# One core, two transformer blocks in float32r: regrouped weight transfers, thin stages as one tile, later turns of x, a reordered stretch of the latent attention, and another matmul order in three tiles

## The reference, cut to what matters

```
mh = rmsnorm(mem, mem_norm);  mk, mv = split(mh @ w_mem_kv)     # first block, memory branch
h  = rmsnorm(x, attn_norm);   proj = h @ w_in ...
u  = causal_dwconv(h2 @ w_up);  x = x + (silu(g) * val) @ w_down
# GLA: q, k, v, gate, gk_low = split(h @ w_in);  gk = gk_low(16 columns) @ w_gk2 + b_gk
# MLA:
proj = h @ w_in                              # 512 | 512 | 64 | 2048 columns
c_q, c_kv, k_rope, gate = split(proj)
q  = (rms_norm(c_q)  @ w_qb ).reshape(S, 16, 128 + 64)    # q_nope | q_rope
kv = (rms_norm(c_kv) @ w_kvb).reshape(S, 16, 128 + 128)   # k_nope | v
q_rope = rope(q_rope);  k_rope = rope(k_rope)
out = causal_softmax(q k) v * silu(gate) @ w_out
```

## Time and profile before

| | us |
|---|---|
| median of 3 runs (2471.82 to 2472.93) | 2472.68 |
| the profiled execution: its own time | 2475.55 |
| its span | 2473.8 |
| TensorE busy in it | 2444.2 (99%) |
| VectorE busy | 1495.6 (60%) |
| ScalarE busy | 1235.7 (50%) |
| mean granted TensorE clock | 0.996 |

### The profile page before, as it was taken

The page is one execution under the profiler, slowest core; times in us unless marked ns, Lnnn a source line. Parts: engine busy times, 40 slices in busy tenths (PEclk is TensorE's granted clock), DMA queues, the critical chain, the costliest instruction groups (busy, mean ns, idle before and its releaser), DMA issues.

```text
span 2473.8 us, 34147 instructions
## 1 busy us (share of the span) xinstructions
PE 2444.2 (99%) x12328; PEld 2070.6 (84%) x12328; DVE 1495.6 (60%) x1842; ACT 1235.7 (50%) x1588; POOL 32.2 (1%) x59
## 2 busy tenths in 40 slices
PE   8999999999999999999999999999999999999998
PEld 7888888888888888888888888888878788789987
DVE  5654544456695565777557765776545555666564
ACT  6544444554445444555445544555454444546553
POOL 2000000000000000000000000000000000000000
PEclk9999999999999999999999999999999999999999
DMA  8565666556566655666666666656655566464554
GB/s 262 175 187 151 205 185 192 160 180 190 161 190 184 211 183 186 184 187 191 195 188 186 185 192 192 185 181 188 173 165 162 178 188 193 124 188 131 159 175 158
DMA packets 421879, 448.29 MB, mean 181 GB/s; under 512 B 30533, under 2 KB 284601, under 8 KB 421250
## 3 DMA queue, kind: packets, MB, share of 16 engines
q1 hardware_dynamic: 419794, 440.80, 59.3%
q0 software_dynamic: 1936, 5.91, 0.9%
q10 hardware_dynamic: 32, 0.01, 0.0%
HBM read 444.55 MB, written 2.10 MB: 181 GB/s over the span
## 4 chain that ended last, share of the span: by engine, by line
PE 94%; DVE 2%; ACT 2%; DMA 1%; SPq 1%; issue 1%; DVEq 0%; ACTq 0%
PE blk L641 88%; PE pa L894 1%; DMA weight_raw<-in_w_mem_kv_dram 1%; DVE weight L1749 1%; ACT weight L1169 1%; PE pa L702 1%; SPq L496 1%; PE pa L679 0%; PE pa L1013 0%; PE pa L693 0%; DVE arena L1749 0%; PE pa L704 0%; PE pa L773 0%; PE pa L791 0%; PE pa L711 0%
## 5 line engine op out<-in xcount | busy, mean ns | idle before, releaser
L1749 DVE TENSOR_TENSOR weight<-weight_raw,weight 128x1024 fp32r<-128x1024 f32 (+2 forms) x840 | 1006.2, 1205 | 736.7 <-ACT weight L1169 732.9
L1169 ACT ACTIVATE weight<-weight_raw 128x1024 fp32r<-128x1024 f32 (+2 forms) x840 | 869.5, 1042 | 747.4 <-PE blk L641 693.6
L641 PE MATMUL blk<-weight,h 128*128 128x512 f32 (+1 forms) x4632 | 1044.6, 386 | 1.5 <-DVE weight L1749 1.5
L641 PEld LDWEIGHTS blk<-weight,h 128*128 128x128 f32 x4632 | 857.1, 188 | 173.9 <-DVE weight L1749 1.9
L641 PE MATMUL blk<-u,weight 128*128 128x512 f32 x3808 | 673.6, 338 | 1.4 <-DVE weight L1749 1.4
L641 PEld LDWEIGHTS blk<-u,weight 128*128 128x128 f32 x3808 | 580.9, 188 | 89.2 <-DVE weight L1749 1.8
L641 PE MATMUL blk<-weight,u 128*128 128x512 f32 x1920 | 448.9, 394 | 1.2 <-DVE weight L1749 0.8
L641 PEld LDWEIGHTS blk<-weight,u 128*128 128x128 f32 x1920 | 361.7, 190 | 78.7 <-DVE weight L1749 2.6
L641 PE MATMUL blk<-h,weight 128*128 128x256 f32 (+1 forms) x896 | 137.5, 316 | 0.8 <-DVE arena L1811 0.8
L641 PEld LDWEIGHTS blk<-h,weight 128*128 128x128 f32 x896 | 124.8, 190 | 13.2 <-DVE weight L1749 1.0
L1749 DVE TENSOR_TENSOR arena<-arena,blk 128x512 f32<-128x512 f32 (+2 forms) x69 | 46.9, 679 | 53.9 <-ACT arena L1542 31.7
(11 more groups left out here) (252 smaller groups left out, 957.2 us busy)
## 6 DMA issues: line engine op xcount, KB each, us to landing
weight_raw<-in_w_in_dram SPq DMA_DIRECT2D x208, 512.0 KB, 3.7
weight_raw<-in_w_up_dram SPq DMA_DIRECT2D x344, 256.0 KB, 3.2
weight_raw<-in_l_gla_w_in_dram SPq DMA_DIRECT2D x96, 512.0 KB, 4.2
weight_raw<-in_w_down_dram SPq DMA_DIRECT2D x84, 512.0 KB, 4.3
weight_raw<-in_w_branch_dram SPq DMA_DIRECT2D x48, 512.0 KB, 4.2
weight_raw<-in_l_mla_w_in_dram SPq DMA_DIRECT2D x48, 512.0 KB, 4.4
weight_raw<-in_w_mem_kv_dram SPq DMA_DIRECT2D x32, 512.0 KB, 5.1
weight_raw<-in_w_out_dram SPq DMA_DIRECT2D x32, 512.0 KB, 4.2
```

Of the source, the lines that this page charges most:

```text
L641: mm = nc.tensor.matmul(to, lhsT, rhs, start=(kt == 0 and m == 0), stop=(kt == ph.bt - 1 and m == len(ops) - 1))
L1169: nc.scalar.activation(hi, raw, ACT.Copy).then_inc(hi_made, 1)
L1749: return nc.vector.tensor_tensor(out_, a, b, op)
```

## The change

- **Transfers.** `heads_from` gives one transfer for all heads of a k chunk: two per tile in place of eight (`qrope`) or four (`v0`, `v1`). The pieces keep their sizes, 256 and 512 bytes.
- **Thin stages.** `decay` and `krope` are one tile of 16 chunks each, and one transfer each. ACT no longer waits, at the start of a thin stage, for the block before it.
- **x turned later.** The turns of x, and their splits, move from steps 0 to 3 of `memv` to steps 2 to 5 (on ACT and DVE 1 to 4 becomes 3 to 6), the norm of `mem_k` three steps later; the turn of `mem_k` stays at step 13.
- **Latent stretch.** `krope` moves behind `qnope0`. The side work is spread anew (below). The evictions of `qnope` and `knope` move from DVE (`copied_to`) to ACT (`columns_to`). `latent`, its junk and `k_rope`/`k_raw` get other places in `arena`.
- **Matmul order.** In the first tile of `sbqk`, `up1` and `up2` (`twos=True`) the matmuls of two chunks are grouped: hi, hi, lo, lo in place of hi, lo, hi, lo. For this the first round of these stages' loop is written out.

```
-        Phase("sbqk", "fm", 8, K16, TC, cols_from(win, 0, K16), "copy"),
+        Phase("sbqk", "fm", 8, K16, TC, cols_from(win, 0, K16), "copy", twos=True),
...
+            Phase(f"up{f}", "fm", nf, K16, TC, pair_from(wup, K16, c0 * P, DFF + c0 * P, P), twos=f > 0),
...
-        Phase("decay", "fmp", 1, K16, DECAY_RANK, cols_from(gla_w_in, 3 * D, K16, DECAY_RANK)),
+        Phase("decay", "fmp", 1, [KD], DECAY_RANK, cols_from(gla_w_in, 3 * D, [KD], DECAY_RANK)),
...
-        Phase("krope", "fmp", 1, K16, LR, cols_from(mla_w_in, 2 * LRANK, K16, LR), "copy"),
...
+        if r == 0:
+            phases += [Phase("krope", "fmp", 1, [KD], LR, cols_from(mla_w_in, 2 * LRANK, [KD], LR), "copy")]
...
-            return [(slice(width * h, width * h + width),
-                     w3[:, 2 * kt:2 * kt + 2, bass.ds(b * (n * per_head) + (first + h) * per_head + at, width)])
-                    for h in range(n)]
+            return [((k, width), w4[:, 2 * kt + k, bass.ds(b * n + first, n), at:at + width]) for k in range(2)]
...
+                        if two_by_two:
+                            ops = [ops[2 * k + m] for q in range(0, nk, 2) for m in range(2) for k in (q, q + 1)]
...
                 steps(pe, plan, ph, 0, side is not None, tile,
-                      from_round=int(ph.t0 == 0 or x_wait is not None))
+                      from_round=int(ph.t0 == 0 or x_wait is not None or ph.twos))
...
             def side_memk(j):
-                if j < 4:
-                    if j == 0:
+                if 2 <= j < 6:
+                    r = j - 2
+                    if r == 0:
                         norm_at(pe, "x", "hn", NT)
...
-            project(PH["krope"], u, side=lambda j: None)
+            project(PH["qrope"], h, x_wait=norm_ready("qa"), side=lambda j: None)
+
+            def side_qnope(j):
+                if j == 1:
+                    turn_latent(1)
 
             def side_krows(j):
-                if j == 1:
+                if j == 0:
                     pe.wait_ge(block_out, PH["krope"].b0 + 1)
...
-                project(PH[f"knope{r}"], h[:, :, KL:2 * KL])
-                project(PH[f"v{r}"], h[:, :, KL:2 * KL])
+                project(PH[f"knope{r}"], h[:, :, KL:2 * KL], side=side_krows if r == 0 else None)
+                project(PH[f"v{r}"], h[:, :, KL:2 * KL], side=(lambda j: turn_k() if j == 1 else None) if r == 0 else None)
...
-                if lift is not None:
+                if lift is not None and ph.kind != "fmp":
                     act.wait_ge(block_out, ph.b0)
...
             def side_kva(j):
                 if j == 0:
+                    latent_rows_sq(1)
+                if j == 2:
                     root("kva")
...
+                project(PH[f"qnope{r}"], columns_to(q_nope),
+                        side=(lambda j: latent_hi(1) if j == 2 else None) if r == 0 else None)
...
+            def side_qrope(j):
                 if j == 1:
+                    rows_inverse_of("kva", LRANK)
+                if j == 3:
                     scale_latent(1)
+                    dve.wait_ge(block_out, PH["qrope"].b0 + 1)
+                    q_rope_part(0)
+            project(PH["qrope"], side=side_qrope)
+
+            def side_qnope(j):
+                if j == 0:
+                    q_rope_part(2)
                 if j == 2:
...
+                    latent_lo(1)
                 if j == 3:
...
+                    dve.wait_ge(block_out, PH["qrope"].b0 + 2)
+                    q_rope_part(1)
+
+            def side_knope(j):
+                if j == 1:
+                    k_rotated()
+                if j == 3:
+                    q_rope_part(3)
```

More of the change, by code:

```diff
@@ L374, in build_program @@
         rstd_rows = small[:, 72:74]
-        latent = area(0, NT, 2 * LRANK)
+        latent, latent_junk = area(10240, NT, 2 * LRANK), area(0, NT, D)
         q_nope, k_nope, l_v = area(0, KW, S), area(2048, KW, S), area(4096, NT, W)
@@ L1102, in side_krows @@
                     mm.then_inc(ML["k_rows"], 1)
-                if j == 2:
-                    turn_latent(1)
-            project(PH["qrope"], h, x_wait=norm_ready("qa"), side=side_krows)
             def turn_k():
@@ L1654, in latent_rows_sq @@
                 for t in range(NT):
-                    nc.scalar.activation(x_junk[:, t, v], latent[:, t, v], ACT.Square,
+                    nc.scalar.activation(latent_junk[:, t, v], latent[:, t, v], ACT.Square,
                                          accum_out=RSTD_COL[n][:, t:t + 1]).then_inc(NORM["sq"], 1)
@@ L1682, in k_lift, with columns_to, go, turned_k_out @@
                 return nc.scalar.activation(k_raw[:, :], blk[:, r, 0, S:2 * S], ACT.Copy)
-            project(PH["krope"], k_lift, side=lambda j: latent_rows_sq(1) if j == 0 else None)
             def side_kva(j):
                 if j == 0:
+                    latent_rows_sq(1)
+                if j == 2:
                     root("kva")
-                if j == 3:
-                    latent_hi(1)
             project(PH["qrope"], rows_to(q_rope), side=side_kva)
+            def columns_to(dst):
+                def go(b, r):
+                    return nc.scalar.activation(dst[:, bass.ds(b * 2, 2), :], blk[:, r, :, 0:S], ACT.Copy)
+                return go
+            def turned_k_out():
+                act.wait_ge(ML["kturned"], 1)
+                nc.scalar.activation(k_rope_even[0:LR], pa[0:LR, 0, 0:S], ACT.Copy).then_inc(ML["kT"], 1)
+                nc.scalar.activation(k_rope_odd[LR:P], pa[LR:P, 0, 0:S], ACT.Copy).then_inc(ML["kT"], 1)
             def round_gated(k):
@@ L2423, in k_out, with k_rotated @@
                 tt(k_raw[:, :], k_raw[:, :], blk[:, r, 0, 0:S], ALU.add).then_inc(block_out, 1)
-            project(PH["krope"], join=k_out, side=lambda j: rows_inverse_of("kva", LRANK) if j == 2 else None)
-            def side_k(j):
+            def k_rotated():
+                dve.wait_ge(ML["k_rows"], 1)
+                link(nc.vector.reduce_sum(k_rope[:, :, 0:LR],
+                                          pa[:, 1, 0:S].rearrange("p (t two d) -> p t d two", t=NT, two=2), AX.X))
+                for t in range(NT):
+                    link(nc.vector.tensor_scalar(k_rope[:, t, 0:LR], k_rope[:, t, 0:LR],
+                                                 RSTD_COL["pre1"][:, t:t + 1], None, ALU.mult))
+                    rope(k_rope[:, t, 0:LR], 1, LR // 2, 2, t, l_rope_a, l_rope_b)
+                nc.vector.tensor_copy(k_rope[:, :, LR:2 * LR], k_rope[:, :, 0:LR]).then_inc(ML["k_roped"], 1)
@@ L2427, in side_k, with q_rope_part @@
+            def q_rope_part(k):
+                t, half = k // 2, k % 2
+                rope(q_rope[:, t, half * 512:(half + 1) * 512], LH // 2, LR // 2, 2, t, l_rope_a, l_rope_b,
+                     ML["q_roped"] if k == 3 else None)
+            def side_qrope(j):
                 if j == 1:
+                    rows_inverse_of("kva", LRANK)
+                if j == 3:
                     scale_latent(1)
-                if j == 2:
-                    dve.wait_ge(ML["k_rows"], 1)
-                    link(nc.vector.reduce_sum(k_rope[:, :, 0:LR],
-                                              pa[:, 1, 0:S].rearrange("p (t two d) -> p t d two", t=NT, two=2), AX.X))
-                    for t in range(NT):
-                        link(nc.vector.tensor_scalar(k_rope[:, t, 0:LR], k_rope[:, t, 0:LR],
-                                                     RSTD_COL["pre1"][:, t:t + 1], None, ALU.mult))
-                        rope(k_rope[:, t, 0:LR], 1, LR // 2, 2, t, l_rope_a, l_rope_b)
-                    nc.vector.tensor_copy(k_rope[:, :, LR:2 * LR], k_rope[:, :, 0:LR]).then_inc(ML["k_roped"], 1)
@@ L2455, in _ @@
             for r in range(2):
-                def q_rope_part(k):
-                    t, half = k // 2, k % 2
-                    rope(q_rope[:, t, half * 512:(half + 1) * 512], LH // 2, LR // 2, 2, t, l_rope_a, l_rope_b,
-                         ML["q_roped"] if k == 3 else None)
-                project(PH[f"qnope{r}"], copied_to(q_nope),
-                        side=lambda j, r=r: q_rope_part(j // 2) if r == 0 and j % 2 == 0 else None)
-                project(PH[f"knope{r}"], copied_to(k_nope),
-                        side=lambda j, r=r: q_rope_part(2) if r == 0 and j == 1 else None)
-                project(PH[f"v{r}"], side=lambda j, r=r: q_rope_part(3) if r == 0 and j == 0 else None)
+                project(PH[f"qnope{r}"], side=side_qnope if r == 0 else None)
+                if r == 0:
+                    project(PH["krope"], join=k_out, side=lambda j: None)
+                project(PH[f"knope{r}"], side=side_knope if r == 0 else None)
+                project(PH[f"v{r}"])
                 def side_mla(j, r=r):
```

69 lines of the change are left out of this document (30 added, 39 removed).

## The result

The changed kernel takes 2455.41 us (median of 4 runs, 2453.62 to 2456.56) and the kernel before, run beside it, 2472.25 (4 runs, 2471.03 to 2472.93): a ratio of 0.9932, 95% interval 0.9915 to 0.9949, or 16.8 us less. I had forecast 12.2 us less; 2455.41 lies 1.6 us under the range. Its profiled execution took 2455.41 us as well (span 2453.7). From profile to profile the difference is 20.1 us, since the profiled execution before, 2475.55, lay 3.3 us above its median.

The account below looks back on a forecast made before the run. TensorE, 99% busy, bounds the kernel; 4.1 + 0.8 + 8.0 = 12.9 us off the profiled 2475.55 gives 2462.6. Against the median 2472.68 it predicted 2460.5 us, 12.2 less, range 2457.0 to 2466.5.

Parts of the forecast that it names:

- Matmul order: First tiles of sbqk, up1 and up2: grouping 48 matmuls wins nothing, term 0, from -0.4 to +0.4 us.
- x turned later: In memv: TensorE's 2.2 us wait for x goes, and 1.9 us of half clock behind it; term 4.1 us.
- mem_k's turn: Turn at memv's step 13, its norm three steps later: 0.9 us to spare, loss taken as 0, up to 1.2 us.
- decay: One tile in place of four thin ones removes TensorE's wait at glav's first tile; term 0.8 us.
- removed ACT wait: ACT no longer waiting at a thin stage's start: no TensorE wait stands there beyond decay, term 0.
- Latent stretch: Stretch of 65.97 us with 57.9 us of TensorE work: waits, half clock and restarts go, term 8.0 us.
- krope's join: DVE joins krope by 2187, asked for at 2187.9: 0.9 us spare, loss taken as 0, up to 1.2 us.
- Rival 1: Half-clock stretches turn up elsewhere or the timed runs lacked them; only waits go, 9.1 us, to 2463.6; chance 0.2.
- Rivals 2 and 3: Second: new DVE or ACT waits, 2465, chance 0.1. Third: long piece lists slow, 2478 or more, chance 0.02 (partial 0.03).

Follow-up runs that it names:

- e1: The changed kernel without the grouped matmul order, first rounds of sbqk, up1 and up2 still written out: 2461.56 us.
- e3: The kernel before with only the grouped first tile of sbqk, up1 and up2, and the first rounds written out for it: 2464.28 us.
- e9: The changed kernel with the turns of x, their splits and the norm of mem_k back at their earlier steps of memv: 2454.43 us.
- e11: The changed kernel with decay as four thin tiles again, krope still one: 2455.05 us.
- e10: The kernel before with only the joined transfers, two for a qrope tile and two for a v tile: 2467.54 us.
- e8: The changed kernel with one transfer for each head again, eight or four a tile: 2454.81 us.
- e5: The changed kernel with the whole of tile 4 grouped in place of tile 0 in sbqk, up1 and up2: 2462.08 us.
- e6: The changed kernel with all 268 tiles of these stages' kind grouped by four chunks (hi x4, lo x4): 2462.22 us.
- e7: The changed kernel with all 268 tiles of these stages' kind grouped by two chunks (hi, hi, lo, lo): 2457.27 us.
- e12: The changed kernel with only the first half (8 matmuls) of tile 0 grouped in sbqk, up1 and up2: 2454.90 us.
- e14: The changed kernel with three of the four chunk pairs grouped in tile 4, in place of tile 0, in the three stages: 2456.27 us, one run.
- e15: The changed kernel with only three of the four chunk pairs grouped in tile 0 of the three stages: 2462.48 us, one run.
- e4: The changed kernel with only the first pair of chunks grouped in the first tile of the three stages: 2461.01 us.
- e13: The changed kernel with tiles 4 to 7 grouped in place of tile 0 in the three stages: 2461.64 us.

## Why the prediction was right in direction and too small

**Matmul order (term 0, -0.4 to +0.4): the step that failed.** It measured 7.4 us in the traces, 6.2 between the medians of e1 and the changed kernel, 8.2 between e3 and before. The prediction took the pace of the alternating order from glaqk, found it as dense as the shapes give, and concluded "Alternation costs nothing". The row was right and was of the wrong stage: glaqk, like up0, had the fast pace from its fourth tile on. One window each in sbqk (60 us), up1 (100) and up2 (80) would have shown 342, 568 and 455 matmuls, where the fast pace has 347, 579 and 464. And the bound of 5% was put on the 48 matmuls that the diff moves, not on the 2240 of the three stages, so the range could not hold it.

**x turned later (4.1): right in this profile, too large for the runs.** Profile to profile it gave 4.0 us. In timed runs nothing of it can be measured: e9, with x early, is 1.0 us below the changed kernel, within the scatter of the runs. Half of the term, 1.9 us, hung on the clock, and the other half on a wait of 2.2 us that three other profiles with x early show as 1.1. mem_k's turn, the thin spot, was in time: its scaling ended at 101.64, and TensorE's turn shows at 102.36 (0.9 us forecast, 0.7 found):

```profile
100.42 1.22 DVE L1760 TENSOR_TENSOR arena<-arena,small 128x1024 f32<-128x1024 f32 x1
```

```profile
102.36 1.91 PE L695 MATMUL pa<-ident,arena 128*128 128x128 f32 x16
```

**decay (0.8): size right, cause wrong.** It gave 1.1 us in the traces, and by e11 this comes from the removed ACT wait, which had the term 0. Both edits are in the change, so the time could not show the wrong cause.

**Latent stretch (8.0): right.** 58.0 us stand where "about 58 us" was forecast, and krope's join, the other thin spot, made no wait. The cause was named in part: the issues of SyncE did hold up the scaling in the old order (e10), but in the new order they would not have (e8). The Trainium skill's rule ("DMA: Bandwidth & Descriptors", Why small descriptors are slow), weighed in the prediction, gives nothing for joining; e10 gives 4.5 us with the pieces unchanged, so in the old order the trace decides against it.

**The rivals.** Rival 1 (the clock does not come back) was half right. The fall at 2175 went; the one at 1816.6 stayed with its place in the program, now at 1804.8. Whether it falls there varies between kernels without an edit near it: behind the 33-row matmuls it fell in the profiles of before, after, e3, e5, e6, e7, e8, e12, e14 and e15 and not in those of e1, e4, e9, e10, e11 and e13. The mean granted clock of each timed run bears on the other half of the rival, that the timed runs did not have the falls. Of the 32 runs of the kernel before beside the experiments, those at 0.996 took 2474.18 to 2475.01 us, those at 0.997 2472.04 to 2473.75, those at 0.998 or 0.999 2469.98 to 2472.85; the profiled execution had 0.996, and one half-clock stretch of 3.4 us lowers the mean by 0.0007. By that measure most timed runs had one to three such stretches fewer than the profiled execution. The Trainium skill says that the point of change differs from run to run ("TensorE: Matmul & The Clock Gate", The HAM clock gate); the runs of this one kernel differ in their mean clock, 0.996 to 0.999, which fits. It is also the likeliest reason that the median fell 16.8 us and the profile 20.1, though no timed run shows which stretch it lacked. Rivals 2 and 3 did not come: there is no new wait, and the weight transfers from the first joined one to 2170 took 2.9 to 5.5 us to land.

**The sum again, with the term put right.** 12.9 + 7.4 = 20.3 off 2475.55 gives 2455.3, against 2455.41 measured. That the profiled execution before lay 3.3 us above its median while the one after lay on its own is why the medians differ by 16.8 only. I had allowed 0.7 us for it (12.9 to 12.2); e1, the change without the matmul order, has its median at 2461.56, 1.1 us above my 2460.5.

## What to carry to other kernels

Where one engine is the bound and 99% busy, count how many instructions it starts in equal windows of every stage of the same kind, not in one: a 2% difference at full clock and without a wait is time to be won, and no list of waits shows it. Price an edit of a stream's order on the whole stage behind it, not on the instructions moved, and test it by moving the edit by one group. Before crediting a removed wait to one of several edits, undo each alone: here two edits cured the same wait, and one cure was enough.

## What the runs showed of the hardware

- A stream of alternating fp32 matmuls of 512 and 256 columns, a new weight load before each, runs in one of two paces, 173.3 or 176.7 ns a matmul on the mean, at full clock, and kept it for as long as the stage lasted (64 tiles, 1024 matmuls). In the kernel before, every stage of this kind that followed 512-column matmuls began slow (sbqk, up0, up1, up2, glaqk, and mlagate1 too); eight transposes behind the first tile left up0 and glaqk slow, four more small matmuls two tiles later made them fast. Grouped by two, a whole tile or half a tile at the start made the three stages fast; one group or three groups at the start did not. From tile 4 on, three groups did, and four or sixteen did not.
- Grouping everywhere is slower than the fast alternation: 2.787 us a tile by two, 2.807 by four, 2.773 alternating.
- SyncE's 40 short transfers took it 23.2 to 23.6 us in either order of the program. In the changed kernel, with two joined ones a tile, TensorE never waited for them.
- Behind a wait of 3.3 us (before) and 3.4 us (e3) for the scaling of the latent the clock fell to half; behind waits of 1.1 us for the scaling of x (e3, e9, e10) it did not, and behind the one of 2.2 us (before) it did.
